# Fused two-block forward pass on Trainium2: 512-column products in the second layer's last feed-forward network of the first block, with VectorE adding the halves

## What is computed

```python
def swiglu_ffn(x, w13, w2):
    a, u = jnp.split(x @ w13, 2, axis=-1)
    return (jax.nn.silu(a) * u) @ w2

    for l in range(DEPTH):            # DEPTH = 2
        h = layer_norm(DEEPNORM_ALPHA * h + 0.5 * swiglu_ffn(h, ffn1_w13[l], ffn1_w2[l]), ...)
        mix = token_mix(h, ...)
        h = layer_norm(DEEPNORM_ALPHA * h + mix, ...)
        h = layer_norm(DEEPNORM_ALPHA * h + 0.5 * swiglu_ffn(h, ffn2_w13[l], ffn2_w2[l]), ...)
    return h[:, N_META:]
```

## Time and profile before

| | |
|---|---|
| median of 3 runs | 1664.33 us (1664.22 to 1664.56) |
| the profiled execution | 1663.59 us, of which the span is 1661.8 us |
| mean granted TensorE clock | 0.995 |
| TensorE busy | 1634.5 us (98%) |
| VectorE busy | 1179.3 us (71%) |
| ScalarE busy | 809.3 us (49%) |
| up stage of the changed FFN, chunks 8 to 20 | 892.2 to 968.9 us |
| its down stage | 969 to 1030 us |

### The profile page before, as it was taken

How to read it: one execution, slowest core, us unless ns; L and a number is a source line. 1 busy time by engine, 2 the same in 40 slices (tenths; PEclk the granted TensorE clock), 3 DMA queues, 4 the chain that set the end, 5 groups by cost and what they waited for, 6 DMA issues and landing times.

```text
span 1661.8 us, 30179 instructions
## 1 busy us (share of the span) xinstructions
PE 1634.5 (98%) x12366; PEld 1549.5 (93%) x12366; DVE 1179.3 (71%) x1636; ACT 809.3 (49%) x1063; POOL 214.1 (13%) x190
## 2 busy tenths in 40 slices
PE   9999999999999999999999999999999999999998
PEld 9999998999999999998999999998988888798887
DVE  6565587795566856577787655787888678788874
ACT  5334375663344533456673344565434446653433
POOL 1001510400033000421030024141000010000000
PEclk9999999999999999999999999999999999999999
DMA  6455453445553555544445554333455543145553
GB/s 236 168 186 200 155 187 132 150 155 177 183 201 136 177 176 187 182 161 157 140 163 205 208 209 174 127 127 127 166 189 196 209 147 133 55 174 177 196 183 127
DMA packets 39153, 279.99 MB, mean 168 GB/s; under 512 B 4880, under 2 KB 6032, under 8 KB 8848
## 3 DMA queue, kind: packets, MB, share of 16 engines
q1 hardware_dynamic: 36896, 270.34, 45.7%
q0 software_dynamic: 2160, 8.29, 1.5%
HBM read 275.10 MB, written 1.05 MB: 166 GB/s over the span
## 4 chain that ended last, share of the span: by engine, by line
PE 85%; DVE 7%; ACT 6%; issue 1%; POOL 1%; DMA 0%; DVEq 0%; SPq 0%; ACTq 0%; POOLq 0%
PE bank L733 21%; PE bank L735 20%; PE bank L734 20%; PE bank L750 8%; PE bank L751 5%; ACT w_hi L1678 3%; DVE w_lo L2384 3%; PE bank L860 1%; PE bank L861 1%; PE bank L866 1%; PE bank L752 1%; ACT h L1738 1%; PE bank L1195 1%; ACT h_both L1737 1%; PE bank L1224 0%
## 5 line engine op out<-in xcount | busy, mean ns | idle before, releaser
L2384 DVE TENSOR_TENSOR w_lo<-raw,w_hi 128x2048 fp32r<-128x2048 f32 (+5 forms) x239 | 562.6, 2355 | 193.2 <-ACT w_hi L1678 192.8
L1678 ACT ACTIVATE w_hi<-raw 128x2048 fp32r<-128x2048 f32 (+5 forms) x247 | 476.0, 1930 | 347.9 <-PE bank L960 122.1
L733 PE MATMUL bank<-h_both,w_hi 128*128 128x272 f32 (+1 forms) x1704 | 490.9, 288 | 2.7 <-DVE w_lo L2384 2.4
L735 PE MATMUL bank<-h_both,w_lo 128*128 128x272 f32 (+1 forms) x1704 | 488.3, 287 | 0.0
L734 PE MATMUL bank<-h_both,w_hi 128*128 128x272 f32 (+1 forms) x1704 | 486.8, 286 | 0.0
L733 PEld LDWEIGHTS bank<-h_both,w_hi 128*128 128x128 f32 x1704 | 321.0, 188 | 6.7 <-DVE w_lo L2384 4.9
L735 PEld LDWEIGHTS bank<-h_both,w_lo 128*128 128x128 f32 x1704 | 321.2, 188 | 0.0
L734 PEld LDWEIGHTS bank<-h_both,w_hi 128*128 128x128 f32 x1704 | 320.8, 188 | 0.1
L733 PE MATMUL bank<-g_both,w_hi 128*128 128x272 f32 (+1 forms) x934 | 269.4, 288 | 2.2 <-ACT vd L2342 1.1
L734 PE MATMUL bank<-g_both,w_hi 128*128 128x272 f32 (+1 forms) x934 | 265.9, 285 | 0.0
L735 PE MATMUL bank<-g_both,w_lo 128*128 128x272 f32 (+1 forms) x934 | 265.6, 284 | 0.0
(11 more groups left out here) (436 smaller groups left out, 2521.0 us busy)
## 6 DMA issues: line engine op xcount, KB each, us to landing
raw<-in_up_w SPq DMA_DIRECT2D x111, 1024.0 KB, 4.8
raw<-in_down_w SPq DMA_DIRECT2D x40, 1408.0 KB, 5.9
raw<-in_in_w SPq DMA_DIRECT2D x20, 1024.0 KB, 4.7
raw<-in_up_w SPq DMA_DIRECT2D x16, 1152.0 KB, 5.1
raw<-in_out_w SPq DMA_DIRECT2D x16, 1024.0 KB, 4.7
raw<-in_even_w SPq DMA_DIRECT2D x12, 1024.0 KB, 4.8
raw<-in_last_down SPq DMA_DIRECT2D x11, 1024.0 KB, 4.8
raw<-in_odd_w SPq DMA_DIRECT2D x6, 1024.0 KB, 5.0
```

The costliest lines, as they stand in the source:

```text
L733: pe.matmul(out, w[0], x[0], start=first, stop=False)
L735: return pe.matmul(out, w[1], x[0], start=False, stop=last)
L1678: last = act.activation(into[:, lo:hi], raw[:, slot, lo:hi], ACT.Copy)
L2384: last = dve.tensor_tensor(lo[:, b:n], raw[:, slot, b:n], hi[:, b:n].bitcast(F32), ALU.subtract)
```

## The change

In this FFN, from chunk 8 on, the up stage's products on TensorE are `mm3_wide` (the half tile's stay `mm3`), and so are those of the down tiles 0 to 6 (tile 7 stays `mm3`). VectorE adds the halves: in the up stage with two `tensor_reduce` a chunk, the gate's sum into `sig` and the up sum into `gf`; ScalarE's silu then works on `sig` in place, and waits for `q_ready` instead of `chunk_used`; the product is one of two SBUF tiles. In the down stage `take_halves` replaces `take_tile`. The last pair of down tiles is written out instead of looped over. The diff, cut to its core:

```diff
@@ TensorE, ffn_down @@
+                        if first.lo and n == T and not (j and isinstance(i, int) and i == KD // 2 - 1):
+                            hi, lo = wpair(slot, k)
+                            both = g_both[:, :, k, META:T]
+                            if k < FT - 2:
+                                mm3_wide(ps[4 + j], (hi, lo), both, k == 0, False)
+                            elif k == FT - 2:
+                                pe.matmul(ps[4 + j][:, 0:S], lo, both[:, 0, :], start=False, stop=False)
+                            else:
+                                pe.matmul(ps[4 + j][:, 0:S], hi, both[:, 0, :], start=False, stop=False)
+                                pe.matmul(ps[4 + j][:, 0:S], lo, both[:, 0, :], start=False, stop=False)
+                                last = pe.matmul(both_halves(ps[4 + j]), wpair(slot, FT - 2)[0],
+                                                 g_both[:, :, FT - 2, META:T], start=False, stop=True)
+                            if isinstance(i, int) and (i, j, k) == (0, 1, 3):
+                                shift()
+                            continue
...
-                looped = KD // 2 if n == T else KD // 2 - 1
+                looped = KD // 2 if n == T and not first.lo else KD // 2 - 1
@@ TensorE, ffn, up @@
+                                if first.lo and (c is None or c >= 8):
+                                    last = mm3_wide(ps[b + e], wpair(slot, 2 * k + e), hboth(k, META),
+                                                    k == 0, k == KD - 1)
+                                    continue
@@ ScalarE, silu @@
+                    if first.lo and norm is not None and (c is None or c >= 8):
+                        act.wait_ge(q_ready, seen.at(q_ready, i * 2 + (j + 1) - 8))
+                        act.activation(sig[:, j, META:], sig[:, j, META:], ACT.Silu).then_inc(silu_ready, 1)
+                        return
@@ VectorE @@
+            def take_halves(k, bank):
+
+                link(dve.tensor_reduce(y[:, k, META:], both_halves(bank), AX.X, ALU.add))
+                if k:
+                    dve.wait_ge(hm_ready, seen.next(hm_ready))
+                dve.tensor_tensor(y[:, k, META:], h[:, k, META:], y[:, k, META:], ALU.add)\
+                    .then_inc(y_ready if k else y0_ready, 1)
@@ VectorE, ffn, up @@
                     b = up_bank(deferred, j, c)
+                    wide = bool(first.lo) and deferred and (c is None or c >= 8)
+                    if wide:
+                        dve.wait_ge(chunk_used, st.value(j, i, 2))
+                        dve.tensor_reduce(sig[:, j, META:], both_halves(ps[b]), AX.X, ALU.add).then_inc(q_ready, 1)
+                        dve.tensor_reduce(gf[:, j, META:], both_halves(ps[b + 1]), AX.X, ALU.add).then_inc(up_free, 1)
                     if deferred and c == 5:
                         split_next(UP_BLOCKS, 0, 7)
                     elif c == UP1 - 1:
...
                     elif c not in ((DEFER, DEFER + 1, 6) if deferred else (0,)):
                         split_next(UP_BLOCKS if c is None else up1_blocks(c + 1), i, j + 1)
...
                     dve.wait_ge(silu_ready, seen.at(silu_ready, nth))
...
+                    if wide:
+                        dve.wait_ge(up_free, seen.at(up_free, nth))
+                        dve.scalar_tensor_tensor(gf[:, j, lo:], sig[:, j, lo:], BRANCH_FFN, gf[:, j, lo:],
+                                                 ALU.mult, ALU.mult).then_inc(dve_seq, 1)
+                        dve.wait_ge(dve_seq, seen.at(dve_seq, i * 2 + (j + 1) - 8))
+                    else:
+                        dve.scalar_tensor_tensor(gf[:, j, lo:n], sig[:, j, lo:n], BRANCH_FFN if n == T else 1.0,
+                                                 ps[b + 1][:, lo:n], ALU.mult, ALU.mult).then_inc(up_free, 1)
+                        dve.wait_ge(up_free, seen.at(up_free, nth))
@@ VectorE, down @@
-                        take_tile(k, ps[4 + k % 2], 1)
+                        if first.lo and k < KD - 1:
+                            take_halves(k, ps[4 + k % 2])
+                        else:
+                            take_tile(k, ps[4 + k % 2], 1)
```

More of the change, by code:

```diff
@@ L746, in mm3_wide @@
             def mm3_wide(bank, w, x, first, last):
-                two = bank[:, :].rearrange("p (a n) -> p a n", a=2)
+                two = both_halves(bank)
                 if not last:
@@ L752, in mm3_wide, with both_halves, hboth @@
                 return pe.matmul(two, w[0], x, start=False, stop=True) if last else lows
-            def hboth(k):
-                return h_both[:, :, k * T:k * T + S]
+            def both_halves(bank):
+                return bank[:, :].rearrange("p (a n) -> p a n", a=2)
+            def hboth(k, lo=0):
+                return h_both[:, :, k * T + lo:k * T + lo + S]
             def chunk_is_split(ahead, pairs=0):
@@ L1886, in ffn @@
                 up1_chunks(act, up, 8 if norm is not None else 2, TAIL_AT[0] - 2)
+                if first.lo and norm is not None:
+                    seen.skip(q_ready, UP1 - 8)
                 st.c += UP1
@@ L2700, in up @@
                     lo = first.lo
-                    dve.scalar_tensor_tensor(gf[:, j, lo:n], sig[:, j, lo:n], BRANCH_FFN if n == T else 1.0,
-                                             ps[b + 1][:, lo:n], ALU.mult, ALU.mult).then_inc(up_free, 1)
-                    dve.wait_ge(up_free, seen.at(up_free, nth))
+                    if wide:
[7 more added lines that the diff above has]
+                        dve.wait_ge(up_free, seen.at(up_free, nth))
                     f = bass.ds(i * 2 + j, 1)
@@ L2733, in ffn @@
                 up1_chunks(dve, up, 8 if deferred else 2, TAIL_AT[0] - 2)
+                if first.lo and deferred:
+                    seen.skip(dve_seq, UP1 - 8)
+                    seen.skip(q_ready, UP1 - 8)
                 for s in (silu_ready, up_free, g_hi_done):
```

## The result

The changed kernel takes 1736.52 us (median of 5 runs, 1735.25 to 1738.76) against 1664.22 us: 1.0444 times the time before, 95% interval 1.0433 to 1.0455. The forecast was 1735.5 us. Its profiled execution has a span of 1734.1 us, 72.3 more than before.

A forecast was written before the change was run, and what follows sets the result against it. TensorE, busy for 98% of the span, was taken as the bound. 1663.6 - 1.4 - 0.5 + 49.1 (stalls) + 24 (clock) = 1734.8, plus 0.7 to the median: 1735.5 us, range 1710 to 1742.

The forecast's parts named there:

- The order of the wait and the split: VectorE, up stage: the split of chunk c+1 can't start until chunk c has ended, when TensorE needs it; 49.1 us.
- The stalls: TensorE idles about 3.6 us ahead of each of chunks 9 to 20 and 3.0 ahead of the down stage; 49.1 us.
- a clock that holds: Rival: the stalls come but TensorE's granted clock does not fall; 1711.5 us, chance 12%.
- Stalls less gain: Up and down stages: 49.1 us of TensorE stalls less 1.9 us won by the wide products.
- The clock: TensorE's clock falls to half behind 12 of 13 stalls, mean 4.5 us, 2.0 us lost each; 24 us.
- the forecast's own price: TensorE at the low clock: 0.213 us a matmul against 0.118, so 45% of the time spent there is lost.
- The wide products' gain: TensorE: 0.11 us a chunk, 1.4 us for 13 up chunks, plus 0.5 us taken for the down stage.
- the case without stalls: Rival: the awaited value is met a chunk earlier, so only TensorE's gain is left; 1662.4 us, chance 3%.
- The covers: Later silu, product, bank release and `take_halves` all hide beside other work; taken at 0 us.
- The tight spot in the down stage: Tile 0: some 0.7 of 0.79 us spare are used up; 0 us taken, 0.1 us once if cover is gone.
- The lower edge of the forecast's own range: Whole kernel: 1730 us, with 20 us for the clock and the down stage's gain at 1.0.
- this rival: TensorE's clock stays low for 6.8 us behind each stall, 40 us instead of 24; 1751.5 us, chance 8%.

The follow-up runs named there:

- e1: The changed kernel with VectorE's wait for chunk c and its two reductions moved behind the split of chunk c+1; 1664.49 us, ratio 1.0005.
- e2: The kernel before, with only VectorE's wait for the end of chunk c added ahead of the split of chunk c+1; 1713.5 us, ratio 1.0301.
- e3: The changed kernel with 14 unread products of 512 columns added on TensorE behind each of chunks 8 to 20; 1712.61 us, ratio 1.0295.
- e6: The kernel of e1 run once more, beside e5 on the same chip; 1664.72 us, ratio 1.0009.
- e5: The change's products with the model network's full order, VectorE splitting chunk c+2 instead of c+1 from chunk 8 on; 1663.32 us, ratio 1.0003.
- e4: The changed kernel with the up stage's wide branches switched off, leaving the down stage's change alone; 1663.2 us, ratio 0.9998.

## Why the prediction was right

**The order of the wait and the split** carried it, and it was read from the code and from the earlier trace rows together: the value awaited is that which released the silus, and the silus stood at the chunk ends. e1 and e2 show it from both sides, by taking the wait away from the wide kernel and by putting it alone into the narrow one.

**The stalls.** Forecast were twelve idle spells of 3.6 us and one of about 3.0; measured 3.58 to 3.85 and 3.04. At a clock that holds, the forecast was 1711.5 us; e3 gave 1712.6. Stalls less gain were put at 49.1 - 1.9 = 47.2 us, and the stretch of e3 shows 49.5. The term that was too small is the restart: behind a wait TensorE's first matmul takes longer than in a dense row. In e3 the second matmul of a chunk starts 0.33 us behind the first (902.23 and 902.56), in a dense row 0.23 us. In e3 there are 5.89 us from a chunk's first matmul to the reduction behind it (902.23 to 908.12), where I had 5.57 + 0.20 = 5.77, and the wait for the split ends some 0.1 us later than the 0.05 taken from the earlier trace rows. Together 0.2 us a stall, the 0.15 to 0.2 that e2 leaves over as well.

**The clock.** 24 us were forecast, 12 falls at the mean length of three in the trace before; e3 puts it at 23.1 us. There were 13 falls, nine of 3.4 and four of 6.8 us, 57.8 us in all and 4.4 us in the mean, nearly as assumed. By the forecast's own price, 45% of the low time, they would cost 26 us. But that price takes all low time for work, and nine of the 13 falls begin while TensorE still stands idle, 0.3 to 1.6 us before it goes on (read in windows of 0.5 us), 7.0 us in all. The rest, 50.8 us, gives 22.9 us, close to the 23.1 of e3. So one fall more than the assumed 12 and idle time that was priced as work cancel, and the mean length came from only three falls: the size was right in part by luck.

The whole kernel lost about 0.5 us less than its stretch (626.29 us from there to the end before, 625.77 after). The clock of the passage behind the down stage was at half for 3.4 us instead of 6.8; but e1 and e6, one kernel, differ by as much there, so it can't be put down to the change.

**The wide products' gain.** 0.11 us a chunk and 0 to 1.0 us for the down stage. e5's chunks in the loop come 5.58 us apart against 5.68, and its up stage ends 1.39 us earlier, which is the forecast gain. The Trainium skill (TensorE: Matmul & The Clock Gate, section "Wait — 56ns, not 53.3ns?") gives about 2.5 ns a matmul, an estimated 0.04 us a chunk; the trace has more than twice that, and it decides. The down tiles take 7.59 against 7.65 us, 0.45 us for seven, and e4's stretch is 0.31 shorter. So the 0.5 us taken fits, but not its source: the 0.007 us a product of the up stage gave 0.14 us a tile, and 0.06 were measured; why stays open. That this adds up to a gain of 1.9 us for the whole kernel, as the case without stalls and the expectations of e1 and e5 said, no run shows; the most that a trace shows is 0.78.

**The covers.** Putting ScalarE's later silu at nothing was right for the changed kernel, where a period has 9 us, and would have been wrong without the stalls: in e1 the same 0.73 us made the next split come at the last moment. The tight spot in the down stage held within 0.1 us: in e4 TensorE's sum of tile 0 starts at 977.68, against 977.78 before.

**The small misses.** The silu of chunk 20 came at 1038.01, 69 us later than before, where 67 were forecast: the restarts. The reductions were to be 9.3 us apart at full clock; e3 shows 9.5. The lower edge of the forecast's own range, 1730, comes to 1731 by its two terms.

The rivals fell as their conditions said. The clock didn't hold. It stayed low for 6.8 us behind four stalls, not all. The argument against this rival had misread its row: the 48 instructions in 10 us are no sparse resumption. TensorE stood idle until 1035.51 and was busy without a break from there on; it made seven matmuls a us there, against eleven once the clock was back at 2.4 GHz. Dense work, as behind the stalls, doesn't exclude the long fall. And the case without stalls would have needed the wait to be met a chunk earlier; e1 comes close to that case, and it came out as no change.

## What to carry to other kernels

When a consumer's new wait for chunk c goes into an in-order engine, look at every instruction behind it and ask for which chunk it works: a preparation for chunk c+1 behind a wait for chunk c puts the two engines in turns. A form that works in one network (here with splits two chunks ahead) can't be moved into another without the lead that it rests on. And where TensorE idles again and again, price the clock as well: here it was a third of the loss, and filling the gaps with useless products brought it back.

## What was not expected of the hardware

- In e2, with eleven idle spells of 2.46 to 2.65 us, one of 2.38 and one of 1.72, the clock fell ten times, each time for 3.4 us. In the changed kernel, with spells of 3.04 to 3.85 us, it fell 13 times of 13, four times for 6.8 us. The longer spells went with more falls and longer ones.
- The length of a spell doesn't settle it. Behind 2.9 us of idle time in the passage to the second block the clock was low for 6.8 us in the trace before and in e6, for 3.4 us in e1 and the changed kernel, and not at all in e5; behind the 2.9 us ahead of the later passage (1160 us) it fell before and held in e1.
- The first matmul behind a wait costs about 0.1 us more than one in a dense row, at full clock (0.33 against 0.23 us to the start of the next; 5.89 against 5.77 us for a chunk).
- Products that nobody reads made the kernel 24 us faster (1712.6 against 1736.5 us), since they kept TensorE at 2.4 GHz.
